# Attention transposes three and weighted values six steps behind the scores; decay rows broadcast from stacked halves; ScalarE splits ahead of its mLSTM root

## The reference

```python
for l in range(2):
    h = modulate(rms_norm(x), sh1, sc1)            # and hc for the context
    mq, mk, mv, mo, mg, aq, ak, av, nq, nk, nv, zg = split(h @ w_in[l])
    y_ml = mlstm_branch(...)     # forward and backward scan with exponential decay per head
    y_ga = gqa_latent(...)       # 8 heads of 64, keys of context and image, softmax, values
    y_na = na_latent(...)        # 8 heads, window bias added to the scores, softmax, values
    o = merge_branches(y_ml, y_ga, y_na, zg)       # sigmoid(zg_b) * (y_b @ w_branch_b), summed, @ w_out
    x = x + ga1 * rms_norm(o)
    x = x + ga2 * rms_norm(conv_ffn(...))
```

## Time and profile before

| | us |
|---|---|
| median of 3 runs | 1825.42 |
| lowest, highest | 1822.68, 1830.49 |
| the profiled execution's own time | 1822.04 |
| its span, first to last instruction | 1820.2 |

### The profile page before, as it was taken

How to read it: one execution, slowest core, us unless ns; L and a number is a source line. 1 busy time by engine, 2 the same in 40 slices (tenths; PEclk the granted TensorE clock), 3 DMA queues, 4 the chain that set the end, 5 groups by cost and what they waited for, 6 DMA issues and landing times.

```text
span 1820.2 us, 27536 instructions
## 1 busy us (share of the span) xinstructions
PE 1726.7 (95%) x10152; PEld 1472.3 (81%) x10152; DVE 1275.8 (70%) x2193; ACT 845.7 (46%) x1336; POOL 591.7 (33%) x360
## 2 busy tenths in 40 slices
PE   7978979999999999999999999999999998999998
PEld 7877878776787777888888887888778888989987
DVE  7889865774668688966788886247735675657873
ACT  6654544455333443344444442345463455556653
POOL 4344424111112212321233323224122233535664
PEclk9989999999999999999999999999999999999999
DMA  8545532232124354442345545223222343535553
GB/s 313 219 149 182 190 116 93 81 105 97 54 93 133 105 168 162 164 149 82 127 139 188 194 185 187 91 75 123 93 76 75 89 164 116 167 119 174 182 192 119
DMA packets 71979, 251.81 MB, mean 138 GB/s; under 512 B 7984, under 2 KB 12336, under 8 KB 71216
## 3 DMA queue, kind: packets, MB, share of 16 engines
q1 hardware_dynamic: 66384, 241.74, 39.6%
q10 hardware_dynamic: 5472, 8.39, 1.4%
HBM read 249.05 MB, written 1.05 MB: 137 GB/s over the span
## 4 chain that ended last, share of the span: by engine, by line
PE 58%; DVE 28%; ACT 7%; issue 5%; DMA 0%; ACTq 0%; POOL 0%; DVEq 0%; POOLq 0%
PE bank L645 45%; DVE w_lo L1637 7%; DVE mod_w L1692 4%; PE bank L776 3%; DVE conv L2499 3%; ACT w_hi L1118 2%; PE bank L956 2%; PE bank L1031 2%; PE bank L933 1%; PE bank L942 1%; DVE probT L1692 1%; PE bank L738 1%; PE bank L1020 1%; DVE att L2169 1%; DVE nbias L2147 1%
## 5 line engine op out<-in xcount | busy, mean ns | idle before, releaser
L599 POOL TENSOR_TENSOR w_lo<-w_raw,w_hi 128x512 fp32r<-128x512 f32 x356 | 591.5, 1673 | 1214.4 <-ACT w_hi L1118 1167.2
L1637 DVE TENSOR_TENSOR w_lo<-w_raw,w_hi 128x512 fp32r<-128x512 f32 x356 | 356.2, 1016 | 291.7 <-ACT w_hi L1118 290.7
L1118 ACT ACTIVATE w_hi<-w_raw 128x1024 fp32r<-128x1024 f32 x356 | 367.7, 1053 | 368.1 <-PE bank L645 266.7
L645 PE MATMUL bank<-hT_hi,w_hi 128*128 128x512 f32 (+1 forms) x1280 | 449.9, 351 | 9.8 <-ACT w_hi L1118 3.6
L645 PE MATMUL bank<-hT_hi,w_lo 128*128 128x512 f32 (+1 forms) x1280 | 439.5, 343 | 0.0
L645 PE MATMUL bank<-hT_lo,w_hi 128*128 128x512 f32 (+1 forms) x1280 | 439.5, 343 | 0.0
L645 PEld LDWEIGHTS bank<-hT_hi,w_hi 128*128 128x128 f32 x1280 | 244.8, 191 | 43.9 <-issue 8.1
L645 PEld LDWEIGHTS bank<-hT_hi,w_lo 128*128 128x128 f32 x1280 | 244.6, 191 | 28.3
L645 PEld LDWEIGHTS bank<-hT_lo,w_hi 128*128 128x128 f32 x1280 | 245.0, 191 | 26.7 <-issue 1.0
L1692 DVE SCALAR_TENSOR_TENSOR mod_w<-mod_w,c_rows 128x1024 f32<-128x1024 f32 x96 | 133.9, 1395 | 1.3 <-DMA mod_w<-in_mod_weights 1.3
L645 PE MATMUL bank<-w_hi,hT_hi 128*128 128x512 f32 x272 | 115.0, 423 | 1.9 <-DVE gkT_lo L2209 1.4
(11 more groups left out here) (357 smaller groups left out, 3086.2 us busy)
## 6 DMA issues: line engine op xcount, KB each, us to landing
w_raw<-in_weights SPq DMA_DIRECT2D x356, 512.0 KB, 4.1
mod_w<-in_mod_weights SPq DMA_DIRECT2D x96, 512.0 KB, 3.8
nbias<-in_window_bias ACTq DMA_DIRECT2D x32, 128.0 KB, 2.4
resid_c<-in_ctx ACTq DMA_DIRECT2D x2, 1024.0 KB, 5.5
c_rows<-in_conditions SPq DMA_DIRECT2D x1, 1024.0 KB, 5.6
gatew<-in_gate_weights SPq DMA_DIRECT2D x1, 1024.0 KB, 12.1
decay<-in_decay SPq DMA_DIRECT2D x1, 1024.0 KB, 5.8
out<-resid_x ACTq DMA_DIRECT2D x2, 512.0 KB, 2.6
```

Of the source, the lines that this page charges most:

```text
L599: nc.gpsimd.tensor_tensor(w_lo[:, s, 0, :], w_raw[:, s, 0:COLS], w_hi[:, s, 0, :].bitcast(F32), ALU.subtract).then_inc(lo0_ready, 1)
L645: mm = pe.matmul(held[key][:, oc], st, mv_, start=(opens and k == 0 and t == 0 and i == 0), stop=(closes and k == tiles - 1 and t == 2), s ...
L1118: a.activation(w_hi[:, p % RING].rearrange("p k n -> p (k n)"), w_raw[:, p % RING, :], ACT.Copy).then_inc(hi_ready, 1)
L1637: v.tensor_tensor(w_lo[:, p % RING, 1, :], w_raw[:, p % RING, COLS:KP * COLS], w_hi[:, p % RING, 1, :].bitcast(F32), ALU.subtract).then_in ...
```

## The change

Four things are changed.

1. In both attentions the transpose comes three steps behind the scores, not two, and the value product six, not four; the streams have three steps more. `turned_of` gives the copied transposes four buffers: `probT` for two of them, and `turned_ga` (where `aq` was) or `turned_na` (in `rows`) for the other two. `turned` waits for the product of two pairs before. Window attention starts after 18 slots and steps every 2 in layer 0 (16 and 2 before), and starts after 8 and steps every 1.8 in layer 1 (8 and 2 before).
2. The decay rows are kept as fp32r, high halves in rows 0 to 35 and low halves in rows 64 to 99 of `rows_hl`, and one fp32r matmul over 100 rows broadcasts their sum; its weights are a column of `sel`, which has ones at the rows of both halves.
3. ScalarE splits weights up to `RING + 1 + l` pieces past the first of the merge before it waits for the sums under the mLSTM root.
4. The unwanted outputs of the modulation products go elsewhere (`junk_of_mod`), because `rows` and `probT` are now in use; three waits guard this in layer 0.

```diff
--- before.py
+++ after.py
@@ -23,7 +23,8 @@
 
 
 
-RET_EVERY, RET_SKIP, GA_EVERY, ML_EVERY, NA_EVERY, NA_SKIP, GA_SKIP, GATE_EVERY = 4, 2, 1, 1, 2, 8, 6, 2
+RET_EVERY, RET_SKIP, GA_EVERY, ML_EVERY, GA_SKIP, GATE_EVERY = 4, 2, 1, 1, 6, 2
+NA_EVERY, NA_SKIP = (2, 1.8), (18, 8)
 
 
 MOD_BLOCKS = 6 * D // P
@@ -246,6 +247,7 @@
     eps = small("eps", [P, 1])
     rows_at = at[0]
     rows = small("rows", [P, 5, TT])
+    sel = small("sel", [P, 2, MH], F32R)
     gain_mix = sb("gain_mix", [P, 2, D], R + 56.0625 * KB)
     gain_ffn = sb("gain_ffn", [P, 2, D], rows_at)
     junk_mix = sb("junk_mix", [P, 4, COLS], R + 16 * KB)
@@ -257,7 +259,11 @@
     onrm = sb("onrm", [P, 2, T], rows_at + 1 * KB)
     mod_w2 = sb("mod_w2", [P, D], rows_at + 4 * KB)
     mod_slot = [mod_w[:, 0, :], mod_w[:, 1, :], mod_w2[:], mod_w3[:]]
-    junk_rows = sb("junk_rows", [P, D], rows_at)
+    turned_ga = sb("turned_ga", [P, 2, TT], S)
+    turned_na = sb("turned_na", [P, 2, TT], rows_at)
+    rows_hl = sb("rows_hl", [P, TT], rows_at + 2 * KB, F32R)
+    junk_gate, junk_ga = sb("junk_gate", [P, D], R + 48.0625 * KB), sb("junk_ga", [P, D], R + 56.0625 * KB)
+    junk_mk = sb("junk_mk", [P, D], R + 24 * KB)
 
     ident = tab[:, TAT["ident"]:TAT["ident"] + P]
 
@@ -337,8 +343,22 @@
         u = unit(s, tts)
         return u if u and u[0] % 2 == 0 else None
 
+    def turned_of(kind, h):
+
+
+        return probT[:, h % 2, :] if h % 4 < 2 else (turned_ga if kind == "ga" else turned_na)[:, h % 2, :]
+
+    def junk_of_mod(m):
+
+
+        if 16 <= m < 24:
+            return junk_nv[:]
+        if 24 <= m < 56:
+            return (junk_mk if m < 26 else junk_gate if m < 32 else junk_ga)[:]
+        return probT[:].rearrange("p a t -> p (a t)")
+
     def steps_of(tts):
-        return range(len(tts) * AH + 3)
+        return range(len(tts) * AH + 6)
 
     def V(name, i=0, n=1):
         return vec[:, VAT[name] + i:VAT[name] + i + n]
@@ -954,7 +974,7 @@
                             for i in range(2):
                                 g = h // 4 if kind == "ga" else h + i
                                 mm = pe.matmul(ps[i * HD:(i + 1) * HD, h // 2 * P:(h // 2 + 1) * P], v_[:, j, g * HD:(g + 1) * HD],
-                                               probT[:, i, j * P:(j + 1) * P], start=(j == 0), stop=(j == n - 1),
+                                               turned_of(kind, h + i)[:, j * P:(j + 1) * P], start=(j == 0), stop=(j == n - 1),
                                                skip_group_check=True)
                         if h == AH - 2:
                             mm.then_inc(*filled((kind, "o", l, t)))
@@ -964,10 +984,10 @@
                     for s in steps_of(q_tts):
                         if pair(s, q_tts):
                             a_scores(*pair(s, q_tts))
-                        if pair(s - 4, q_tts):
-                            a_out(*pair(s - 4, q_tts))
-                        if unit(s - 2, q_tts):
-                            a_turn(*unit(s - 2, q_tts))
+                        if pair(s - 6, q_tts):
+                            a_out(*pair(s - 6, q_tts))
+                        if unit(s - 3, q_tts):
+                            a_turn(*unit(s - 3, q_tts))
                         yield
 
 
@@ -1006,10 +1026,8 @@
 
                     for d in range(2):
                         ps = take(pe, ("mb", l, h, d), "side")
-                        r = 32 * d + h
-                        mm = pe.matmul(ps[:, qs],
-                                       tab[0:GATE_ROWS, TAT["ident"] + r:TAT["ident"] + r + 1].to_broadcast([GATE_ROWS, P]),
-                                       rows[0:GATE_ROWS, 4, qs], start=True, stop=True)
+                        n = 64 + GATE_ROWS
+                        mm = pe.matmul(ps[:, qs], sel[0:n, d, h:h + 1].to_broadcast([n, P]), rows_hl[0:n, qs], start=True, stop=True)
                         mm.then_inc(*filled(("mb", l, h, d)))
 
                 def ml_scores(h, s):
@@ -1076,7 +1094,7 @@
                         mm.then_inc(*filled(("my", l, h)))
 
 
-                na = Beside(attention("na", nv, nprob), NA_EVERY, NA_SKIP if last else 2 * NA_SKIP)
+                na = Beside(attention("na", nv, nprob), NA_EVERY[l], NA_SKIP[l])
                 merge(0, na)
                 merge(1, na)
                 na.finish()
@@ -1410,13 +1428,13 @@
                         A.mark(exp_done, (kind, l, h, t))
 
                     def turned(h, t):
-                        if h >= 2:
-                            act.wait_ge(*probT_used.at((kind, l, h // 2 * 2 - 2, t)))
+                        if h >= 4:
+                            act.wait_ge(*probT_used.at((kind, l, h // 2 * 2 - 4, t)))
                         elif t > q_tts[0]:
-                            act.wait_ge(*filled_at((kind, "o", l, t - 1)))
+                            act.wait_ge(*(filled_at((kind, "o", l, t - 1)) if h >= 2 else probT_used.at((kind, l, AH - 4, t - 1))))
                         ahead((kind, "t", l, h, t))
                         act.wait_ge(*filled_at((kind, "t", l, h, t)))
-                        a.activation(probT[:, h % 2, 0:keys(t)], psum((kind, "t", l, h, t))[:, 0:keys(t)], ACT.Copy)\
+                        a.activation(turned_of(kind, h)[:, 0:keys(t)], psum((kind, "t", l, h, t))[:, 0:keys(t)], ACT.Copy)\
                             .then_inc(*A.drain((kind, "t", l, h, t)))
 
                     def result(t):
@@ -1427,10 +1445,10 @@
                             .then_inc(*A.drain(key))
 
                     for s in steps_of(q_tts):
-                        if unit(s - 2, q_tts):
-                            turned(*unit(s - 2, q_tts))
-                        if pair(s - 4, q_tts) and pair(s - 4, q_tts)[0] == AH - 2:
-                            result(pair(s - 4, q_tts)[1])
+                        if unit(s - 3, q_tts):
+                            turned(*unit(s - 3, q_tts))
+                        if pair(s - 6, q_tts) and pair(s - 6, q_tts)[0] == AH - 2:
+                            result(pair(s - 6, q_tts)[1])
                         if pair(s, q_tts):
                             h, t = pair(s, q_tts)
                             exponential(h, t)
@@ -1521,6 +1539,7 @@
                 evac_tok(("nv", l), tts, lambda t, ps: (nv[:, t, :], ps[:]), beside=ml)
                 evac_T(("nq", l), nqT_hi, scale=float(HD) ** -0.5, beside=ml, halves=True)
                 ml.finish()
+                split_hi(piece("w_in_2", l, 9) + RING + 1 + l)
                 act.wait_ge(*ml_ss.at(l))
                 a.activation(rs[:, 8:24], ss[:, 8:24], ACT.Sqrt).then_inc(*A.tell(ml_root, l))
                 def mlstm_T():
@@ -1550,6 +1569,8 @@
                             else:
                                 if half:
                                     act.wait_ge(*gate_used.at((l, b, 0, g)))
+                                elif b == 1 and l == 0 and g == 0:
+                                    act.wait_ge(mod_used, 32)
                                 elif b == 2:
                                     act.wait_ge(*gate_used.at((l, 1, 1, g)))
                                 dst = ptmp[:, g * per:(g + 1) * per, t0:TT]
@@ -1590,7 +1611,7 @@
                         src = by_half(merged, k, t0) if half else merged[:, k, t0:TT]
                         a.activation(dst, src, ACT.Copy, scale=0.5).then_inc(*A.tell(merged_hi, (l, k)))
 
-                na = Beside(attention("na", y_na, nprob), NA_EVERY, NA_SKIP if last else 2 * NA_SKIP)
+                na = Beside(attention("na", y_na, nprob), NA_EVERY[l], NA_SKIP[l])
                 merge(0, na)
                 merge(1, na)
                 merge(2)
@@ -1688,7 +1709,7 @@
                         dve.wait_ge(mod_used, m)
                     for s in range(sets):
                         w = mod_slot[slot]
-                        product = w if s == sets - 1 else junk_nv[:] if m in range(16, 24) else junk_rows[:] if m in range(24, 56) else probT[:].rearrange("p a t -> p (a t)")
+                        product = w if s == sets - 1 else junk_of_mod(m)
                         mm = v.scalar_tensor_tensor(product, w, 1.0, c_rows[:, s, :], ALU.mult, ALU.mult,
                                                     accum_out=modT[:, l, j, s:s + 1])
                         mm.then_inc(*(W.next() if s < sets - 1 else (mod_used, 1)))
@@ -2137,6 +2158,9 @@
                     dve.wait_ge(*W.last())
 
                 dve.wait_ge(tab_loaded, 16)
+                if l == 0:
+                    ones = [ident[:, o:o + 64].rearrange("p (d r) -> p d r", d=2)[:, :, 0:MH] for o in (0, 64)]
+                    v.tensor_tensor(sel[:], ones[0], ones[1], ALU.add).then_inc(*W.next())
 
                 def load_bias(i):
 
@@ -2234,6 +2258,7 @@
                     v.memset(rows[0:G, 4, :], 0.0).then_inc(*W.next())
                     yield
                     dve.wait_ge(*W.last())
+                    v.memset(rows_hl[32:64, :].bitcast(F32), 0.0).then_inc(*W.next())
```

(10 more changed lines are left out.)

## The result

The changed kernel takes 1810.1 us (median of 5 runs, 1807.1 to 1811.8), the one before 1823.7 (5 runs, 1822.3 to 1830.5): a ratio of 0.9917, interval 0.9896 to 0.9939, or 13.6 us less. The forecast was 1793, some 31 us less. The profiled execution took 1811.1 us, 11.0 less than the profiled one of before. So I explain 11 to 14 us, and the 17 us or more that did not come.

What follows compares the result with a forecast made beforehand. TensorE, busy 1726.7 of 1820.2 us, was taken as the bound. Gains 9.1 + 2.5 + 1.5 + 8.5 + 10.5 = 32.1 us off 1822.0 gave 1789.9, plus 3.4 for the median: 1793, range 1787 to 1801 (chance 0.55).

Steps and rivals of the forecast that it cites:

- Decay rows: mLSTM stages: one fp32r matmul per row saves 5.8 us in layer 0 and 3.3 in layer 1, 9.1 in all.
- TensorE hardly waits here: First mLSTM stage: TensorE busy 105.2 of 107 us, so the whole 9.1 us of the decay rows was taken.
- Root: Layer 1's merge: splits ahead of the root shorten TensorE's wait by 2.0 us, plus 0.5 for the clock: 2.5.
- In layer 0 ... nothing: Layer 0 before the root: ScalarE idles 6.1 us, a split and the table load fit, so no gain.
- Grouped attention: Both layers: of 4.0 us of waits at scores and product, 1.5 us gained; ends 0 and 4.0.
- First window attention: Layer 0: 5.2 us of waits, 1.8 for yT_lo and 1.5 of clock go, 8.5 in all; ends 3 and 10.2.
- Second window attention: Layer 1: 7.5 of 8.1 us of waits and 3.0 of 3.4 of clock go, 10.5; ends 4 and 11.5.
- VectorE is busy 46 of 73, no cap: Second window attention: VectorE busy 46 of 73 us, so it would not limit the 10.5 us gain.
- The clock: Low-clock losses behind waits: 1.7 us in the first window attention, 3.4 in the second; 1.5 and 3.0 counted as gained.
- VectorE takes over: Rival, chance 0.17: TensorE meets VectorE's full queue at the maxima instead of the transpose; gain 18.1 us, 1807.
- Behind 956 and 933 under 1 us per attention: Sign: TensorE's waits at value products (956) and scores (933) fall under 1 us in each attention.
- Some 9 us shorter in each window attention: Sign: the stretches of each window attention become some 9 us shorter.

Runs made afterwards that it cites:

- x6_sigmoid: The changed kernel with ScalarE's sigmoid of zo moved behind the mLSTM steps, ahead of the split and the root: 1807.1 us.
- x8_oldlag: The changed kernel with the old lags (transposes two steps behind, value products four) and two buffers; decay rows, root and pace kept: 1811.7 us.
- x7_shortmods: The changed kernel with modulation products 24 to 55 run over 64 of 1024 columns, leaving out most of their VectorE work: 1804.4 us.
- x13_spread2: The changed kernel with the sigmoid behind the mLSTM stage, yT_lo subtractions spread in both layers, layer 0's second-merge modulation rows begun four slots later: 1798.2 us.
- x3: The kernel before with the attention's part alone (longer lags, four buffers, new start and pace), decay rows and root as before: 1820.6 us.
- x11: The kernel before with only the later start of window attention in layer 0 (18 instead of 16 slots): 1823.2 us.
- x1: The kernel before with the stacked fp32r decay rows alone: 1820.9 us.
- x2: The kernel before with ScalarE's splits ahead of the mLSTM root alone: 1820.5 us.
- x12: The kernel before with only the denser pace of window attention in layer 1 (every 1.8 instead of 2 slots): 1824.5 us.

## Why the prediction was wrong

By its own steps, with the gains of the profile of the changed kernel:

- **Decay rows**, 9.1 forecast, 5.6 measured (3.3 and 2.3). The price of a row was right (0.47 us for a pair). The step that failed is "TensorE hardly waits here", taken from a busy share of 105.2 in 107 us: that was true only while the fp32 rows hid the exponents. I had written that the exponents "lose 0.7 us of cover" and gave it no price. It is 2.56 us at the first head behind the sigmoid (0.9 before), and 1.7 at the second, where VectorE makes the projection's low half first. With the sigmoid moved (x6_sigmoid) the stages gain 9.2, so most of what was missing stood behind a queue, not in the matmuls.
- **Root**, 2.5 forecast, 2.0 measured; the wait changed its name to `w_lo` and lasts 2.0 us, as forecast. The clock drop behind it stayed (at 1438 the clock is at its lower level for 3.4 us), so the 0.5 for it did not come. The step that failed is "In layer 0 ... nothing": the earlier splits bring VectorE's work forward there, and the kernels that have them gain 1.8 to 2.2 us more in the first window attention than those with the new start but without them.
- **Grouped attention**, 1.5 forecast, 0.5 + 0.7 measured, each below what I read in one column.
- **First window attention**, 8.5 forecast, 5.3 measured, some 3.5 of it the later start and the rest, as far as the traces tell, the splits ahead of the root. The step that failed is the 5.2 us of waits that the lag was to take away: it took none. With the lag TensorE waits 4.9 us in this stretch, without it (x8_oldlag) 4.6, and the gains are 5.3 and 5.4. VectorE's 64 of 70 us was named as the cap, and then given too little weight. With the load taken off (x7_shortmods) the stretch gains 10.9, with the lag in place.
- **Second window attention**, 10.5 forecast, 2.9 measured (4.4 in the second profile), the step that failed most. Of the 7.5 us of waits that were to go, the lag brought 1.3 to 2.4 us and the pace 0.8 to 1.5; of the 3.0 for the clock nothing came in the first profile. "VectorE is busy 46 of 73, no cap" reads a mean where the order counts. The branch sums that made the transpose wait 3.72 us didn't go with the lag; they stayed in VectorE's queue, one step earlier or later, ahead of some maxima. The transpose is now three steps behind and doesn't care, but the scores have only two banks, and their wait for the exponentials closes a loop of its own (scores, maxima, exponentials, bank free) in which no transpose stands. The forecast for these scores, that ScalarE's split comes sooner, missed that ScalarE waits for VectorE here (4.34 us), not for TensorE.
- **The clock**: 1.7 + 3.4 us of drops were to go, and those two went; the second came back at 1485 to 1495 in the new wait, for 6.8 us as before (3.4 in the second profile). The up-projection's drop, 5.1 us (3.5 in the second profile), was in no rival; the profile of before happened to have none there. Time at the lower level was 33.7 us before and is 52.1 in the changed kernel, 30.3 in x13_spread2.

The sum: 5.6 + 2.0 + 1.2 + 5.3 + 2.9 = 17.0, less 0.7 at the start and 5.1 in the up-projection, 11.2 against the 11.0 of the table. The rival "VectorE takes over" told the mechanism nearly in its words, "VectorE's full queue, at the maxima instead of the transpose", and its 1807 is 3 us off; its own terms were 9.1 + 1 + 0 + 3 + 5 = 18.1. I gave it 0.17, because the second window attention spoke against it, where it is not the load but the order of the queue. Of the sights that were to show it, the decay rows' spacing, the empty wait for `nprob` at the transposes, the merge's 2 us for `w_lo` and the full clock at 570 and 1525 came true, and two did not. "Behind 956 and 933 under 1 us per attention": the products are clean, the scores wait 11.1 us over four attentions. "Some 9 us shorter in each window attention": 5.3 and 2.9.

What is open: how often the clock falls at the first up-projection of layer 1 in the timed runs. It does in eleven traces (both of the changed kernel, x3 to x11), and not in seven (three of before, x1, x2, x12, x13), and only one execution per run was traced. The profiled execution of before, without the fall, is 3.4 us under the median of its three runs, and that of the changed kernel, with it, 1.0 above its own. It is also open what the splits ahead of the root gain in layer 0 by themselves.

## What to carry to other kernels

A longer software pipeline can move a wait instead of removing it, when the engine in the middle works its queue in order. Here the lag gave nothing in one window attention and some 2 us in the other, of 12.7 us of waits that it was to take away. So before lengthening a lag, follow the loop with the fewest buffers (here two score banks) through every queue it passes, and look at what stands ahead of its link in each. A busy share answers whether an engine has room, not whether it has it in time; a block of 2.5 us in a queue that was 65% busy cost the second window attention 1.2 to 1.6 us at equal clock, and 4.0 where the clock fell with it. And when an operation gets shorter, ask what it was covering: here 3.5 of 9.1 us went into waits, the longest behind a sigmoid with two table loads, and came when that was moved. Last, before two traces are compared stretch by stretch, compare the time that each spent at the lower clock there: a fall that comes or not is worth as much as the edits tried here.

## What the runs showed of the hardware

A table load holds ScalarE for 1.28 us and no longer: the next instruction starts right behind it, at 438.94 + 1.28 = 440.22 (shown 440.23) and at 442.17 + 1.28 = 443.45 (443.46). The Trainium skill ("ScalarE: Activation LUTs", What ACT_TABLE_LOAD costs) puts a switch at about 2.66 us with a drain; by it the pair around the sigmoid would have taken 2 x 1.38 = 2.8 us more, an estimate from the page's figure. The trace shows none of that, and the measurement decides.

TensorE's clock was at its lower level for 13.7 us on end while TensorE's row shows it busy 14.00 of 14.00 us, with no wait of its own there (the row 1595 to 1609 above), and at full clock at the same place in seven other traces. A full busy row is therefore no sign of full clock. The clock changed only at certain instants, a fixed step apart within a trace, and it fell there when such an instant came 0.05 to 2.26 us behind the end of a wait of 1.95 us, and not when it came 2.92 us or more behind. Why it then stayed low for 10.2 or 13.7 us of full rows, no run of this case shows.
